# Joining the high and low halves of the moving operand into one 512-column matmul, for the token group of 256

## The reference, cut to what matters

```python
h = layer_norm(ALPHA * x + y, ln1_g[i], ln1_b[i])
r = jax.nn.relu(h @ mlp_w1[i])
f = (r * r) @ mlp_w2[i]
e = (p[i] @ ple_w[i]) * jax.nn.sigmoid(h @ ple_gate_w[i])
x = layer_norm(ALPHA * h + f + e, ln2_g[i], ln2_b[i])
```

## Time and profile before

| | |
|---|---|
| three runs | 2252.51, 2252.55, 2255.11 us |
| median | 2252.55 us |
| the profiled execution | 2255.11 us, span of the program 2253.3 us |
| instructions in the span | 31627 |
| granted TensorE clock, mean | 0.988 |

### The profile page before, as it was taken

How to read it: one execution, slowest core, us unless ns; L and a number is a source line. 1 busy time by engine, 2 the same in 40 slices (tenths; PEclk the granted TensorE clock), 3 DMA queues, 4 the chain that set the end, 5 groups by cost and what they waited for, 6 DMA issues and landing times. The chain is left out here.

```text
span 2253.3 us, 31627 instructions
## 1 busy us (share of the span) xinstructions
PE 2167.7 (96%) x13166; PEld 2146.6 (95%) x13166; DVE 1263.4 (56%) x1827; ACT 813.9 (36%) x1237; POOL 70.7 (3%) x61
## 2 busy tenths in 40 slices
PE   8999999999999999999899998998899999999996
PEld 8999999999999999999889998997799999999996
DVE  4333357687454434346677755776666346444576
ACT  3222123545333222223444433445244234333342
POOL 0000000000000000000300010000200000000000
PEclk9999999999999999999999999999999999999998
DMA  4011131334223111111122332333122111222232
GB/s 164 29 56 47 47 131 51 114 110 141 65 83 112 38 38 57 38 48 56 47 85 81 128 122 94 126 117 108 54 83 93 57 47 51 71 76 75 85 113 87
DMA packets 62495, 181.76 MB, mean 81 GB/s; under 512 B 13344, under 2 KB 21152, under 8 KB 62368
## 3 DMA queue, kind: packets, MB, share of 16 engines
q1 hardware_dynamic: 60288, 179.82, 24.5%
q10 hardware_dynamic: 2080, 0.12, 0.1%
HBM read 175.46 MB, written 4.46 MB: 80 GB/s over the span
## 5 line engine op out<-in xcount | busy, mean ns | idle before, releaser
L663 PE MATMUL ps<-h_hi_lo,w_split 128*128 128x400 f32 (+1 forms) x2160 | 706.4, 327 | 37.9 <-ACT y_scaled_t L888 23.7
L665 PE MATMUL ps<-h_hi_lo,w_split 128*128 128x400 f32 (+1 forms) x2160 | 705.1, 326 | 0.0
L664 PE MATMUL ps<-h_hi_lo,w_split 128*128 128x400 f32 (+1 forms) x2160 | 705.0, 326 | 0.0
L663 PE MATMUL ps<-r_hi_lo,w_split 128*128 128x400 f32 (+1 forms) x1632 | 535.2, 328 | 16.3 <-DVE acc L1154 16.3
L664 PE MATMUL ps<-r_hi_lo,w_split 128*128 128x400 f32 (+1 forms) x1632 | 531.8, 326 | 0.0
L665 PE MATMUL ps<-r_hi_lo,w_split 128*128 128x400 f32 (+1 forms) x1632 | 531.2, 325 | 0.0
L1154 DVE TENSOR_TENSOR acc<-acc,ps 128x400 f32<-128x400 f32 (+1 forms) x768 | 379.0, 518 | 151.5 <-PE ps L665 148.4
L663 PEld LDWEIGHTS ps<-h_hi_lo,w_split 128*128 128x128 f32 x2160 | 412.1, 191 | 44.4 <-issue 34.7
L586 DVE TENSOR_TENSOR w_split<-w_raw,w_split 128x1024 fp32r<-128x1024 f32 x298 | 363.8, 1239 | 160.5 <-ACT w_split L787 160.4
L787 ACT CAST w_split<-w_raw 128x1024 fp32r<-128x1024 f32 x298 | 305.8, 1047 | 351.9 <-PE ps L665 351.5
L665 PEld LDWEIGHTS ps<-h_hi_lo,w_split 128*128 128x128 f32 x2160 | 413.2, 191 | 0.0
(11 more groups left out here) (80 smaller groups left out, 1115.5 us busy)
## 6 DMA issues: line engine op xcount, KB each, us to landing
w_raw<-w_stream SPq DMA_DIRECT2D x322, 512.0 KB, 3.4
x_raw<-x_t SPq DMA_DIRECT2D x4, 704.0 KB, 6.9
w_raw<-p_t SPq DMA_DIRECT2D x4, 352.0 KB, 3.5
y_t<-acc SPq DMA_DIRECT2D x2, 704.0 KB, 5.1
y_t<-acc SPq DMA_DIRECT2D x4, 352.0 KB, 2.6
x_raw<-x_t SPq DMA_DIRECT2D x2, 512.0 KB, 8.3
y_t<-acc SPq DMA_DIRECT2D x2, 512.0 KB, 5.7
w_raw<-p_t SPq DMA_DIRECT2D x2, 256.0 KB, 3.1
```

Of the source, the lines that this page charges most:

```text
L663: pe.matmul(out, wh, mov_h, start=first, stop=False)
L664: pe.matmul(out, wh, mov_l, start=False, stop=False)
L665: return pe.matmul(out, wl, mov_h, start=False, stop=last)
```

## The change: what it does

Two constants are changed.

```diff
-JOINED = (False, False, False)
+JOINED = tuple(2 * t <= 512 for t in T)
...
-MM_US, ADD_US, GATE_US, R_LO_US, SPLIT_US = (0.167, 0.124, 0.167), (0.57, 0.42, 0.57), (0.62, 0.43, 0.62), (0.66, 0.46, 0.66), 1.23
+MM_US, ADD_US, GATE_US, R_LO_US, SPLIT_US = (0.167, 0.124, 0.167), (0.57, 0.86, 0.57), (0.62, 0.43, 0.62), (0.66, 0.85, 0.66), 1.23
```

## The result

The changed kernel takes 2327.04 us (median of 4 runs, 2326.0 to 2328.66), before 2252.53 in the same session: a ratio of 1.0328, 95% interval 1.0310 to 1.0347. It is 74.5 us slower; 23.5 us had been forecast, and the range ended at 2296. The profiled execution took 2336.38 us, span 2334.6, 81.3 us more than before's; it is slower than the four timed ones, so differences between the two profiled executions come out some 7 us larger than those of the medians.

The account below looks back on a forecast made before the run. TensorE (PE), busy 96% of the span, was taken as the bound, others mattering where they make it wait. Terms -7.7 + 17.1 - 0.3 + 3 + 2 + 5.5 + 4 = +23.6 us on 2252.5 gave 2276 us, range 2252 to 2296.

Parts of the forecast that it names:

- the term for the dense stretches: Visits among norms, pooling and MLP: VectorE's extra 4.0 us a visit mostly falls into idle time; +4, between -6 and +12.
- signs of being wrong: VectorE starting additions sooner than 2.36 us behind PE, or idle PE from 1000 to 1800 us changing far over 10 us.
- PE's saving: Joined pair instead of triple saves 10 ns (bounds 0 and 40); outside "down" and "gate", 768 x 0.010 = -7.7 us.
- Rivals 1 (40 ns saved): Fewer instructions are worth more on PE: 40 ns saved each, sum -5, 2247 us; chance 0.08.
- 4 (nothing saved): Rival: nothing saved or lost on PE, sum +31, 2284 us; a bound inside the mechanism's 0.70, no chance of its own.
- The reduction's price: VectorE's new reduction of 2 x 256 from PSUM: between 0.42 and 0.69 us, taken as 0.68.
- "down" of group 1: Fifth block waits for a bank freed late by VectorE's additions; +0.57 us in each of 30 pairs of steps, +17.1.
- "gate" of layer 1: Group 1's gates, with a norm hung on them: 7 or 8 reductions of 0.72 us straight on the path, +5.5.
- "gate" of layer 0: Group 1's gates: the sigmoid-to-sigmoid ring through ScalarE and VectorE grows from 3.46 to 4.2 us, partly hidden; +2.
- "up" of group 1: The reduction before Relu delays the low part 0.7 us; shows only in 9 visits with a refill, +0.33 each, +3.
- Rival 2: The new constants relieve the dense stretches: +4 becomes -24, sum -4, 2248 us; chance 0.10.
- Rival 3: Side work slips too far: layer 1's group 1 gates wait for their norm, clock may fall; +10 to +20, chance 0.10.

Follow-up runs that it names:

- e3: Joined form in the "down" steps of group 1 alone, old constants, against the kernel before: 2275.03 us, ratio 1.0093.
- e6: e3 with the first "down" block's two additions moved ahead of the low part of the "up" before it: 2258.18 us, 1.0021 of the kernel before.
- e1: The change with the planner's old constants, so only the joined form for group 1, against the kernel before: 2320.41 us, ratio 1.0297.
- e4: Joined form everywhere in group 1 except the "down" steps, old constants, against the kernel before: 2296.76 us, ratio 1.0194.
- e5: e4 with the second "up" tile's reduction moved right behind the first tile's low part, ahead of splits and side work: 2275.21 us, 1.0094 of the kernel before.
- e12: The kernel before plus three unneeded VectorE additions behind the low part of each "up" step of group 1: 2262.92 us, ratio 1.0039.
- e2: Triples everywhere, with only the planner's new constants, against the kernel before: 2262.54 us, ratio 1.0039.
- e7: e1 with three VectorE reorderings (early reduction, early first "down" block, gates' weight split and side work later): 2280.24 us, 1.0116 of the kernel before.
- e11: Joined in input projections, "out" and calm group 1 "up" and "down", early reduction and first block, old constants, against the kernel before: 2245.71 us, 0.9962.
- e9: e11 with the gates' weight split and side work also held behind the "ple" multiplication and accumulation: 2239.85 us, 0.9937 of the kernel before.
- e8: The kernel before (triples) with only the gate steps' weight split and side work held behind the "ple" multiplication and accumulation: 2245.90 us, 0.9964.

## Where the prediction was wrong, and what in it was right

The forecast was 2276 us with a range to 2296; measured were 2327. The way was right, the size was not: the term for the dense stretches failed, and the sum had none for the clock. Two of its own signs of being wrong came: PE's waits on the additions are 58.9 us (33.7 + 25.2) where some 35 were forecast, and PE's idle time from 1000 to 1800 us went from 48 to 82.

**PE's saving: a third too large.** PE's timeline after, group 1's part of one pass of the projections in (24 pairs, between 60.66 and 69.29 us before):

```profile
60.59 0.39 PE L670 MATMUL ps<-x_hi_lo,w_split 128*128 128x512 f32 x1
...
69.06 0.35 PE L663 MATMUL ps<-x_hi_lo,w_split 128*128 128x400 f32 x1
```

8.47 us for 24 pairs are 353 ns each, forecast 349 to 351; 8.63 us for 24 triples were 360. So 7 ns are saved and not 10, and the term -7.7 becomes some -5. Rivals 1 (40 ns saved) and 4 (nothing saved) are out. By the rule of the Trainium skill quoted in the prediction ("TensorE: Matmul & The Clock Gate", Back-to-back issue gap), which the page gives for an isolated matmul, a pair would take 325 ns; the trace of after disagrees as that of before did.

**The reduction's price: right.** 688 ns, taken 0.68. The other end, 0.42, is out; that the operation runs at the single rate (the Trainium skill, "VectorE: DVE Perf Modes", The perf-mode tier table) agrees with it.

**"down" of group 1: right.** +17.1 forecast; e3, which also has its share of dense visits, costs 22, and the pair of steps takes 6.43 us, worked out as 6.44. Shown by e6, which takes most of it away.

**"gate" of layer 1: right** (+5.5, measured +5.0 in after, e1, e4 and e5). **"gate" of layer 0: too small.** The sigmoids follow each other as forecast; ScalarE after:

```profile
549.58 0.42 ACT L904 ACTIVATE t<-t 128x256 f32<-128x256 f32 x1 [0.42 <-DVE t L941]
...
553.82 0.42 ACT L904 ACTIVATE t<-t 128x256 f32<-128x256 f32 x1 [0.41 <-DVE t L941]
```

4.24 us apart, forecast 4.2. But 4.0 us show in e4 and not 2. PE has to wait 1.6 us behind the third tile, since the second tile's reduction stands behind a norm's "lo" pass of 3.48 us (the mechanism of "up" again), and then some 0.6 us a tile for the ring. The new constants hang another norm's pass into this ring, for another 6.

**"up" of group 1 and the dense stretches: here it failed.** The term +3 was for nine "down" steps behind a refill. Four of them are in calm visits and cost 0.2 us once and 0.83 three times in e4, for 0.33 each; the other five stand in dense ones. There +4 became +33.0 in e4, and in after, where 7 of its "down" term belong, +41.9. The step that failed is "each visit brings VectorE 8 x 0.33 + 2 x 0.68 = 4.0 us more", of which "Most falls into its idle time". It counted the reduction as load. But VectorE's queue is in order, and the reduction stands ahead of Relu: so the whole chain of ScalarE for the second tile, which ran beside VectorE's side work, now waits until that work is done and then runs alone. While it runs VectorE idles (1.37 us for each tile of the example), and this idle time takes up no load, since what is queued behind has to wait too. e5 and e12 show it, one by the same work in another place, the other by about as much work that ScalarE does not wait for. The prediction had followed exactly this order for a step with a split between; it did not ask what the same chain does with a norm's pass of 3.5 us in the split's place, though only 18 of the 64 "up" steps of group 1 have any side work and could have been gone through one by one.

**Rival 2** (the constants relieve the dense stretches) is half true: -6.1 us there in e2, and more than that lost in the gates and at the pooling. **Rival 3** was near to e2's loss, which comes from a norm's piece in a gate step, but in layer 0, not in layer 1, and of a norm that these gates do not need.

**The clock: not in the sum.** Only rival 3 said that it may fall. It fell with the stalls, 0.988 to 0.976 on the whole, and by e4's example that adds 1.6 us to a stall of 3.64. PE is busy 19.1 us longer, although 1408 pairs save 9 us at 7 ns. So some 28 of the 81.3 us are matmuls run at the lower clock; that is an estimate from these numbers, and it is spread over the other terms.

What stays open: how the last 31 us of e7's dense visits divide between load and order (e5, with a part of its changes, has +16.6 there). No version was tried that plans the side work anew for the joined form with the order of e7.

## What to carry to other kernels

An instruction added to an in-order queue costs more than its length when another engine's chain hangs on it: ask what stands ahead of it in that queue in every step, the longest piece above all, and whether the chain ran beside that piece before. Free time of an engine, as an average, says nothing of that. When the saving is small (7 ns in 360) and the price is a second read of PSUM, use the form only in steps where nothing waits, and free the first bank ahead of work that waits for others; that, with before's constants, turned +3.3% into -0.4% (e11), and -0.6% with a reordering of the gates (e9) that is worth 0.4% to the triples too (e8).

## What was not expected of the hardware

A shorter stall was followed by as low a clock as a longer one: in e5 PE stalls 2.20 us and the granted clock of the next 6.00 us is 0.72, the same as behind e4's stall of 3.64 us. Behind e12's stall of 1.11 us at the same place it stays 1.00. Windows of e5, then of e12:

```profile
1198.99:1204.99 6.00, 6.00 (x25) 5.96 (x25) 3.01 (x6) 4.08 (x7) 0.00 (x0) 0.72 0.00 0
```

```profile
1199.24:1203.70 4.46, 4.46 (x25) 4.45 (x25) 3.01 (x6) 3.23 (x6) 0.00 (x0) 1.00 0.01 4
```

So e5 gave back 1.44 us of e4's stall and none of the 1.6 us that follow it.
